# Seven products for eight in the first FFN products of a two-layer encoder step, with six load buffers, split weight sums, and a third slot in the last products

## The chip, the cores and the metric

The kernel runs on one core of one Trainium2 chip. The metric is device time in microseconds (us) from start to end of the launch; less is better. TensorE is called PE, VectorE DVE, ScalarE ACT, GpSimd POOL and SyncE SP.

## What is computed

Two groups of tokens (512 of a prompt, 8 x 16 of samples; together 640, as five tiles of 128) pass through two layers. Each layer is FFN, mixer, FFN, and each of these has an RMSNorm ahead of it and one behind it. Everything is fp32.

```
x = x + 0.5 * rmsnorm(swiglu(rmsnorm(x, g0), w_in, w_out), g1)
x = x + rmsnorm(mixer(rmsnorm(x, g2)), g3)          # layer 0: RG-LRU and FoX attention; layer 1: differential attention
x = x + 0.5 * rmsnorm(swiglu(rmsnorm(x, g4), w_in, w_out), g5)

swiglu(x, w_in, w_out):  g, u = split(x @ w_in);  return (silu(g) * u) @ w_out
# d_model 1024, d_ff 2816: w_in is 1024 x 5632, w_out is 2816 x 1024
```

So there are four FFNs, f = 0 to 3. The change touches them alone.

## The kernel before

**Precision.** Each fp32 product is made of three matmuls on fp32r parts: every operand is split into a high part (ACT copies it to fp32r, `act_hi`) and a low part (DVE subtracts the high part from the original, `dve_lo`), and PE adds low times high, high times low and high times high in PSUM.

**First products (A0 to A3, `pe_pairs`).** The 2816 hidden columns are 22 chunks of 128. For each chunk there are two weight tiles of 1024 x 128, one for the gate and one for the up half. The weights stand still in PE and the transposed tokens (`xT_hi`, `xT_lo`) stream past, in two pieces of 384 and 256 columns (tiles 0 to 2, tiles 3 and 4). That is 2 tiles x 8 blocks of the contraction x 3 parts x 2 pieces = 96 matmuls a chunk. ACT takes Silu of the gate's PSUM (`act_ffn`), DVE multiplies it with the up half's into the hidden state `hid` (`dve_ffn`). The weight tiles come through four load buffers `raw` (SP's queue, `sp_unit`) and two split slots (`w_slot`; the first two of a stage have slots apart).

**Last products (B0 to B3, `pe_ffn_out`).** Here a chunk of `hid` stands still and a row of 1024 weights streams past. A first group makes tiles 0 to 2 in 22 units (18 matmuls of 512 columns each, a loop), then a second group makes tiles 3 and 4 in 22 units (12 matmuls each, `pe_second_group`), while the norm of tiles 0 to 2 is taken on DVE, ACT and POOL (`dve_norm_first`, `act_norm_first`, `pool_norm`). Each unit's row and its piece of `hid` are split again, into one of two slots: unit u may be split once unit u - 2 is through PE. The last two units go through PE together (`pe_last_units`), so that tile 3 is ready before tile 4.

**Between stages.** With the last units running, ACT and DVE split the first tiles of the next stage, then finish the norm of tiles 3 and 4 (`act_norm_rest`, `dve_norm_rest`). PE transposes the normed tiles (`pe_xt`), ACT copies them out of PSUM as `xT_hi` and DVE subtracts for `xT_lo` (`act_xt`, `dve_xt`). The first products of a stage begin with tiles 0 to 2 while tiles 3 and 4 are still being normed.

Each engine runs its own list of instructions in order, with semaphores between engines; nothing reorders them.

## Time and profile before

| what | value |
|---|---|
| time, median of 3 runs | 2756.61 us (2749.81 to 2757.88) |
| the profiled execution: its own time, its span | 2743.6 us, 2741.5 us |
| PE busy | 2585.1 us, 94% of the span |
| DVE, ACT, POOL busy | 1146.5 us (42%), 865.4 us (32%), 120.1 us (4%) |
| granted clock of PE, mean | 0.979 |
| DMA | 260.93 MB, 95 GB/s over the span |

A busy PE in this profile is one that has matmuls in flight; their ends are modelled, so the distance from one start to the next tells what a matmul costs, not its own length. The profiled execution was 13 us shorter than the median of the runs.

### The profile page before, as it was taken

How to read it: one execution, taken by the hardware profiler on the slowest of the kernel's cores; microseconds unless marked ns; L12 is line 12 of the kernel's file. 1: busy time of each engine (PE TensorE's matmuls, PEld its weight loads, DVE VectorE, ACT ScalarE, POOL GpSimd, SP SyncE). 2: the span in 40 equal slices, each digit the busy share in tenths (PEclk: the TensorE clock that was granted, in tenths of full speed). 3: DMA queues.
4: the chain of work that ended last, by engine and by line, in shares of the span. 5: the costliest groups of instructions: out<-in, count | busy, mean ns of one | idle time of the engine just before them, and what ended most of it. 6: DMA issues, size and time to landing. Idle time of an engine off the chain costs nothing.

```text
span 2741.5 us, 38402 instructions
## 1 busy us (share of the span) xinstructions
PE 2585.1 (94%) x14963; PEld 2323.5 (85%) x14963; DVE 1146.5 (42%) x1739; ACT 865.4 (32%) x1427; POOL 120.1 (4%) x177
## 2 busy tenths in 40 slices
PE   6999999998889999999999999999996699999998
PEld 6999987886768999987799998777784479999986
DVE  3222246666556222235522223553247853222355
ACT  3112235344344222124422113442233442112243
...
GB/s 151 77 77 70 76 128 148 112 69 70 78 16 133 83 70 75 77 99 138 169 63 76 77 77 103 137 129 131 66 163 41 19 120 85 77 76 70 97 127 158
DMA packets 259061, 260.93 MB, mean 95 GB/s; under 512 B 25567, under 2 KB 213999, under 8 KB 258976
## 3 DMA queue, kind: packets, MB, share of 16 engines
...
## 4 chain that ended last, share of the span: by engine, by line
PE 83%; DVE 10%; ACT 3%; issue 2%; POOL 1%; DMA 1%; ACTq 0%; SPq 0%; DVEq 0%
PE ps L530 16%; PE ps L532 16%; PE ps L531 16%; PE ps L571 7%; PE ps L573 7%; PE ps L572 7%; PE ps L885 2%; DVE w_all L400 2%; PE ps L887 2%; PE ps L886 2%; ACT w_all L394 2%; PE ps L1361 1%; PE ps L1065 1%; PE ps L815 1%; DVE small L1420 1%
## 5 line engine op out<-in xcount | busy, mean ns | idle before, releaser
L400 DVE TENSOR_TENSOR w_all<-raw,w_all 128x1024 fp32r<-128x1024 f32 (+1 forms) x460 | 521.4, 1134 | 999.8 <-ACT w_all L394 679.3
L394 ACT ACTIVATE w_all<-raw 128x1024 fp32r<-128x1024 f32 (+1 forms) x460 | 453.8, 987 | 1521.2 <-PE ps L532 946.2
L530 PE MATMUL ps<-xT_hi,w_all 128*128 128x384 f32 (+1 forms) x2784 | 859.4, 309 | 2.0 <-DVE w_all L400 2.0
L532 PE MATMUL ps<-xT_hi,w_all 128*128 128x384 f32 (+1 forms) x2784 | 858.6, 308 | 0.0
L531 PE MATMUL ps<-xT_lo,w_all 128*128 128x384 f32 (+1 forms) x2784 | 858.5, 308 | 0.0
L530 PEld LDWEIGHTS ps<-xT_hi,w_all 128*128 128x128 f32 x2784 | 527.2, 189 | 2.2 <-DVE w_all L400 2.2
L531 PEld LDWEIGHTS ps<-xT_lo,w_all 128*128 128x128 f32 x2784 | 527.4, 189 | 0.0
L532 PEld LDWEIGHTS ps<-xT_hi,w_all 128*128 128x128 f32 x2784 | 527.2, 189 | 0.0
L571 PE MATMUL ps<-w_all 128*128 128x512 f32 x848 | 336.1, 396 | 17.4 <-DVE w_all L415 17.1
L572 PE MATMUL ps<-w_all 128*128 128x512 f32 x848 | 330.7, 390 | 0.0
L573 PE MATMUL ps<-w_all 128*128 128x512 f32 x848 | 330.5, 390 | 0.0
L481 DVE TENSOR_TENSOR arena<-silu,ps 128x384 f32 (+3 forms) x176 | 85.8, 488 | 369.8 <-PE ps L532 368.1
L571 PEld LDWEIGHTS ps<-w_all 128*128 128x128 f32 x848 | 159.1, 188 | 68.2 <-DVE w_all L415 35.0
L573 PEld LDWEIGHTS ps<-w_all 128*128 128x128 f32 x848 | 159.2, 188 | 34.3
L572 PEld LDWEIGHTS ps<-w_all 128*128 128x128 f32 x848 | 159.3, 188 | 30.4
L885 PE MATMUL ps<-w_all,xT_lo 128*128 128x512 f32 x354 | 141.9, 401 | 14.4 <-ACT tok L953 8.0
L886 PE MATMUL ps<-w_all,xT_hi 128*128 128x512 f32 x354 | 138.0, 390 | 0.0
L887 PE MATMUL ps<-w_all,xT_hi 128*128 128x512 f32 x354 | 138.0, 390 | 0.0
L716 POOL TENSOR_SCALAR small<-small 128x1 f32<-128x1 f32 x60 | 21.8, 364 | 2070.5 <-ACT scratch L662 2020.3
L885 PEld LDWEIGHTS ps<-w_all,xT_lo 128*128 128x128 f32 x354 | 66.4, 188 | 37.2 <-DVE w_all L400 17.1
L415 DVE TENSOR_TENSOR w_all<-arena,w_all 128x384 fp32r<-128x384 f32 (+1 forms) x176 | 85.4, 485 | 0.0
L410 ACT ACTIVATE w_all<-arena 128x256 fp32r<-128x256 f32 (+2 forms) x176 | 79.8, 453 | 0.0
...
## 6 DMA issues: line engine op xcount, KB each, us to landing
raw<-in_w_ffn_in SPq DMA_DIRECT2D x176, 512.0 KB, 3.8
raw<-in_w_ffn_out SPq DMA_DIRECT2D x176, 512.0 KB, 3.6
...
raw<-in_w_out_even SPq DMA_DIRECT2D x16, 512.0 KB, 3.6
raw<-in_w_out_odd SPq DMA_DIRECT2D x16, 512.0 KB, 3.7
gain<-in_norm_g POOLq DMA_DIRECT2D x12, 512.0 KB, 5.3
...
raw<-in_w_in_even SPq DMA_DIRECT2D x8, 512.0 KB, 4.0
```

The costliest lines, as they stand in the source:

```text
L394: return nc.scalar.activation(w_slot(u, it, n)[0], raw[:, u % 4, 0:n], ACT.Copy)
L400: return nc.vector.tensor_tensor(lo, raw[:, u % 4, 0:n], hi.bitcast(F32), ALU.subtract)
L481: nc.vector.tensor_tensor(dst, silu[:, half, 0:w], pair_bank(c, 1, half, w), ALU.mult).then_inc(h_done, 1)
L530: nc.tensor.matmul(dst, wl, xh, start=(k == 0), stop=False)
L531: nc.tensor.matmul(dst, wh, xl, start=False, stop=False)
L532: mm = nc.tensor.matmul(dst, wh, xh, start=False, stop=(k == KD - 1))
L571: nc.tensor.matmul(dst, xl, wh[:, cols], start=start, stop=False)
L572: nc.tensor.matmul(dst, xh, wl[:, cols], start=False, stop=False)
L573: mm = nc.tensor.matmul(dst, xh, wh[:, cols], start=False, stop=stop)
L885: nc.tensor.matmul(dst, xl, wh, start=(k == 0), stop=False)
L886: nc.tensor.matmul(dst, xh, wl, start=False, stop=False)
L887: return nc.tensor.matmul(dst, xh, wh, start=False, stop=(k == KD - 1))
```

## The change

The first products of an FFN become, for each chunk, a product of 2 x 2 blocks: the gate and the up tile are each halved along the contraction (four weight quarters of 512 x 128), and the tokens are halved along contraction and along tokens (four quarters of 512 x 320). Winograd's form of Strassen's scheme makes the four result blocks (gate and up, tokens 0 to 319 and 320 to 639) out of seven products of 4 blocks x 3 parts = 12 matmuls of 320 columns, so 84 matmuls a chunk. In PSUM the products that share a sum are added in place.

- **Token operands.** The transposed tokens are copied unsplit to `xs`; seven operands are made of them once for an FFN (B11, B21, B22 and the differences T1 to T4), each 128 x 1280, and each is split into `xb`. The `xT` and `tok` tiles now lie in the room of `xb`.
- **Weight operands.** For each chunk there are four sums of quarters, S1 to S4, made in place in the load buffers: S3 and S1 on POOL (`pool_sums`), S2 and S4 on DVE (`dve_sums`). Each of the seven operands (128 x 512) is split by ACT and DVE into a ring: four places apart for the first four, then five in turn (`w_ring`).
- **Results.** ACT copies three partial sums out of PSUM (P1, then P1+P6, then P1+P6+P7), DVE adds three times, ACT takes Silu twice, DVE multiplies twice; all of 320 columns.
- **Loads.** Six buffers serve the FFN's first products; the two new ones are the tile `gain`, whose norm gains are now loaded after the products.
- **Order.** `SEQUENCE` lists the 154 products of an FFN; every engine walks it. A product's operand is prepared up to five products ahead, its result is taken five steps later. The first products are no longer a loop.
- **Third slot.** In the second group of the last products the units use three slots in turn, one of them in `xb`, which is free by then (`late_slot`).

```diff
+SEQUENCE = [(name, j) for name in ("P1", "P2", "P5", "P6", "P7", "P4", "P3") for j in range(2)]
+SEQUENCE += [(name, j - back) for j in range(2, KF + 1)
+             for name, back in (("P1", 0), ("P5", 0), ("P4", 1), ("P6", 0), ("P2", 0), ("P3", 1), ("P7", 0))
+             if 2 <= j - back < KF]
+RING, AHEAD = 5, 4
+XOF = {"P1": "B11", "P2": "B21", "P3": "B22", "P4": "T4", "P5": "T1", "P6": "T2", "P7": "T3"}
...
+        def raw_buf(b):
+            return raw[:, b, :] if b < 4 else gain[:, b - 4, :]
...
+        def late_slot(u0, k, n=None):
+            g0, g1 = HALVES[1][0], TOK
+            if k % 3 == 0:
+                b = 0 if late_ffn(u0) in (1, 3) else 8
+                t = [xb[:, b + i].rearrange("p k n -> p (k n)").rearrange("p (a n) -> p a n", n=g1 - g0) for i in range(2)]
...
+        def act_hi_late(act, u0, k):
...
+            act.wait_ge(used, v - 2 if k else v - KF)
...
+        def act_operand(act, f, i):
+            name, j = SEQUENCE[i]
+            summed = {"P7": s3_done, "P5": s1_done, "P6": s2_done, "P3": s4_done}.get(name)
+            if summed is not None:
+                act.wait_ge(summed, KF * f + j + 1)
+            else:
+                pair_wait(act, f, j, 1 if name == "P4" else 0)
+            if i >= AHEAD + RING:
+                act.wait_ge(prod_mm, NPROD * f + i - RING + 1)
...
+            nc.scalar.activation(w_ring(i)[0], operand_raw(f, name, j), ACT.Copy).then_inc(op_hi, 1)
...
+        def pool_sums(pool, f, j):
+            a11, a12, a21, a22 = quarters(f, j)
+            g = KF * f + j
+            pool.wait_ge(op_lo, NPROD * f + PLACE["P1", j] + 1)
+            pair_wait(pool, f, j, 1)
+            nc.gpsimd.tensor_tensor(a11, a11, a21, ALU.subtract).then_inc(s3_done, 1)
+            pool.wait_ge(s3_done, g + 1)
+            nc.gpsimd.tensor_tensor(a21, a21, a22, ALU.add).then_inc(s1_done, 1)
...
         def dve_ffn(dve, f, p, nxt):
+            for i in range(AHEAD, NPROD + RING + 4):
+                if i == 4:
+                    dve.wait_ge(xt_hi, XT["pre%d" % (BEFORE[f] + 1)] + NT)
+                    dve_t(dve, f, "T1")
+                    dve_t(dve, f, "T3")
+                    dve_xb(dve, f, "T1")
+                if i == 5:
+                    dve_t(dve, f, "T2")
+                if i == 6:
+                    dve_xb(dve, f, "T2")
+                if i == 8:
+                    dve_t(dve, f, "T4")
+                    dve_xb(dve, f, "T3")
...
+                if i < NPROD:
+                    dve_operand(dve, f, i)
+                    dve_sums(dve, f, i)
...
+                if 0 <= i - RING < NPROD:
+                    dve_after(dve, f, i - RING)
+                if 0 <= i - RING - 3 < NPROD:
+                    dve_up(dve, f, i - RING - 3)
...
+        def pe_pairs_ffn(pe, f, meanwhile=None):
...
+                if i == AHEAD:
+                    pe_xt(pe, pre_, 3, 3)
+                    pe_xt(pe, pre_, 4, 4)
+                    pe.wait_ge(xt_hi, XT[pre_] + 4)
+                pe.wait_ge(op_lo, NPROD * f + i + 1)
+                if j == 0:
+                    pe.wait_ge(xb_lo_done, 7 * f + XB_ORDER.index(XOF[name]) + 1)
...
+                for k in range(HK):
...
+                    nc.tensor.matmul(dst, wl, xh[:, k, :], start=first, stop=False, skip_group_check=True)
+                    nc.tensor.matmul(dst, wh, xl[:, k, :], start=False, stop=False, skip_group_check=True)
+                    mm = nc.tensor.matmul(dst, wh, xh[:, k, :], start=False, stop=(k == HK - 1), skip_group_check=True)
```

**Where instructions stand.** The first place is DVE's list inside the first products. Before, two chunks are six rows: two products into `hid` (in `arena`) and one split a weight tile.

```order
L481 TENSOR_TENSOR arena<-silu,ps 128x384
L481 TENSOR_TENSOR arena<-silu,ps 128x256
L400 TENSOR_TENSOR w_all<-raw,w_all 128x1024
L481 TENSOR_TENSOR arena<-silu,ps 128x384
L481 TENSOR_TENSOR arena<-silu,ps 128x256
L400 TENSOR_TENSOR w_all<-raw,w_all 128x1024
```

After, one chunk in the middle of a stage is fourteen rows, of which the first twelve stand here with their waits (`gain` and `raw` are load buffers; L591 splits an operand, L616 and L620 are S2 and S4, L674, L667, L678 and L670 take results).

```order
L591 TENSOR_TENSOR w_all<-gain,w_all 128x512 [waits op_hi]
L674 TENSOR_TENSOR arena<-scratch,ps 128x320 [waits prod_mm,silu1_done]
L591 TENSOR_TENSOR w_all<-gain,w_all 128x512 [waits op_hi]
L616 TENSOR_TENSOR gain<-gain 128x512 [waits s3_done,op_lo]
L591 TENSOR_TENSOR w_all<-raw,w_all 128x512 [waits op_hi]
L667 TENSOR_TENSOR scratch<-scratch,ps 128x320 [waits prod_mm,p1_done]
L591 TENSOR_TENSOR w_all<-gain,w_all 128x512 [waits op_hi]
L678 TENSOR_TENSOR arena<-arena,ps 128x320 [waits prod_mm,u2_done]
L591 TENSOR_TENSOR w_all<-gain,w_all 128x512 [waits op_hi]
L620 TENSOR_TENSOR gain<-gain 128x512 [waits s2_done,op_lo]
L670 TENSOR_TENSOR arena<-arena,ps 128x320 [waits u3_done]
L591 TENSOR_TENSOR w_all<-raw,w_all 128x512 [waits op_hi]
```

One more split and the second product into `hid` follow. Between the first and the third row POOL makes S3 and S1, and ACT copies S1's high part: the third row waits for that.

The second place is PE's list at the start of a stage. Before, the transposes of tile 3 (`tok`) come after two products of 24 matmuls:

```order
L530 MATMUL ps<-xT_hi,w_apart 128x384
L531 MATMUL ps<-xT_lo,w_apart 128x384
L532 MATMUL ps<-xT_hi,w_apart 128x384
L815 MATMUL ps<-con,tok 128x128 x8
L530 MATMUL ps<-xT_hi,w_all 128x384
L531 MATMUL ps<-xT_lo,w_all 128x384
```

After, those of tiles 3 and 4 come together after four products of 12 matmuls, and the product behind them is P5, the first that needs tokens of both halves:

```order
L842 MATMUL ps<-xb,w_apart 128x320
L840 MATMUL ps<-xb,w_apart 128x320
L841 MATMUL ps<-xb,w_apart 128x320
L842 MATMUL ps<-xb,w_apart 128x320
L1195 MATMUL ps<-con,tok 128x128 x16
L840 MATMUL ps<-xb,w_all 128x320
L841 MATMUL ps<-xb,w_all 128x320
```

So the products that may run ahead of the late tiles are fewer matmuls than before (48 of 320 columns, where 72 of 384 stood before tile 4's transposes).

The third place is ACT's list where the second group of the last products begins. Before, each split of a row (L394) and of its piece of `hid` (L410) goes to `w_all`:

```order
L394 ACTIVATE w_all<-raw 128x1024 [waits used,raw_in2]
L410 ACTIVATE w_all<-arena 128x256
L662 ACTIVATE scratch,small<-ps 128x1024 [waits ss_x_done,m_mm]
L662 ACTIVATE scratch,small<-ps 128x1024 [waits ss_m_done,m_mm]
L394 ACTIVATE w_all<-raw 128x1024 [waits used,raw_in3]
L410 ACTIVATE w_all<-arena 128x256
```

After, the first unit and every third one go to `xb`, and the norm's rows (L1012) stand where they stood:

```order
L538 ACTIVATE xb<-raw 128x1024 [waits used,raw_in2]
L539 ACTIVATE xb<-arena 128x256
L1012 ACTIVATE scratch,small<-ps 128x1024 [waits ss_x_done,m_mm]
L1012 ACTIVATE scratch,small<-ps 128x1024 [waits ss_m_done,m_mm]
L538 ACTIVATE w_all<-raw 128x1024 [waits used,raw_in3]
L539 ACTIVATE w_all<-arena 128x256
```

## Rows read from the trace of the kernel before

**Rows 1.** The page: busy time of TensorE, and the chain's shares by engine.
```profile
PE 2585.1 (94%) x14963; PEld 2323.5 (85%) x14963; DVE 1146.5 (42%) x1739; ACT 865.4 (32%) x1427; POOL 120.1 (4%) x177
PE 83%; DVE 10%; ACT 3%; issue 2%; POOL 1%; DMA 1%; ACTq 0%; SPq 0%; DVEq 0%
```

**Rows 2.** Windows: busy us and instructions by engine, granted clock, DMA share, GB/s.
```profile
889.70:890.30 0.60, 0.60 (x9) 0.60 (x7) 0.60 (x1) 0.00 (x0) 0.18 (x1) 1.00 0.12 36
...
881.00:1192.00 311.00, 311.00 (x2127) 310.90 (x2126) 82.74 (x95) 67.01 (x97) 5.63 (x8) 1.00 0.27 79
1192.00:1282.00 90.00, 90.00 (x401) 74.51 (x400) 38.24 (x46) 34.33 (x48) 0.80 (x2) 1.00 0.40 123
1282.00:1356.00 74.00, 66.18 (x291) 51.39 (x290) 49.41 (x57) 38.81 (x59) 10.32 (x12) 1.00 0.54 166
2664.00:2735.00 71.00, 63.28 (x264) 48.08 (x262) 40.25 (x49) 31.09 (x47) 2.12 (x5) 1.00 0.49 156
```

**Rows 3.** Timeline of TensorE, one chunk of A0: start us, us, instruction.
```profile
101.07 0.34 PE L530 MATMUL ps<-xT_hi,w_all 128*128 128x384 f32 x1
...
105.23 0.28 PE L530 MATMUL ps<-xT_hi,w_all 128*128 128x256 f32 x1
...
108.10 0.34 PE L530 MATMUL ps<-xT_hi,w_all 128*128 128x384 f32 x1
...
115.13 0.34 PE L530 MATMUL ps<-xT_hi,w_all 128*128 128x384 f32 x1
```

**Rows 4.** Groups by line and shape: busy us and mean ns, idle before.
```profile
L400 DVE TENSOR_TENSOR w_all<-raw,w_all 128x1024 fp32r<-128x1024 f32 x382 | 467.7, 1225 | 869.8 <-ACT w_all L394 549.5 <-ACT w_all L410 320.0
L400 DVE TENSOR_TENSOR w_all<-raw,w_all 128x512 fp32r<-128x512 f32 x78 | 53.7, 690 | 130.0 <-ACT w_all L394 129.8
L394 ACT ACTIVATE w_all<-raw 128x1024 fp32r<-128x1024 f32 x382 | 404.7, 1060 | 1357.1 <-PE ps L532 934.4 <-PE ps L573 398.8 <-DVE arena L481 21.2
L394 ACT ACTIVATE w_all<-raw 128x512 fp32r<-128x512 f32 x78 | 49.1, 630 | 164.0 <-PE ps L887 152.3 <-PE ps L532 11.7
L481 DVE TENSOR_TENSOR arena<-silu,ps 128x384 f32 x72 | 39.9, 554 | 148.3 <-PE ps L532 148.3
L415 DVE TENSOR_TENSOR w_all<-arena,w_all 128x256 fp32r<-128x256 f32 x88 | 36.9, 419 | 0.0
L410 ACT ACTIVATE w_all<-arena 128x256 fp32r<-128x256 f32 x88 | 35.3, 401 | 0.0
```

**Rows 5.** Timeline of TensorE in B1's second group: waits before units, in brackets.
```profile
1289.26 0.50 PE L571 MATMUL ps<-w_all 128*128 128x512 f32 x1 [0.76 <-DVE w_all L415]
...
1296.39 0.50 PE L571 MATMUL ps<-w_all 128*128 128x512 f32 x1 [1.38 <-DVE w_all L415]
...
1350.26 0.50 PE L587 MATMUL ps<-w_all 128*128 128x512 f32 x1 [3.11 <-DVE w_all L415]
```

**Rows 6.** Timeline in B0's second group: GpSimd beside VectorE.
```profile
430.30 0.55 POOL L720 TENSOR_TENSOR small<-small 128x1 f32<-128x1 f32 x1
...
436.92 1.28 DVE L741 SCALAR_TENSOR_TENSOR x<-tok,small,x 128x1024 f32<-128x1024 f32 x1
437.13 2.94 POOL L720 TENSOR_TENSOR small<-small 128x1 f32<-128x1 f32 x1
```

**Rows 7.** Timeline at the start of A1: tile 4, and the table load.
```profile
889.33 1.28 DVE L751 SCALAR_TENSOR_TENSOR tok<-x,small,gain 128x1024 f32<-128x1024 f32 x1 [0.44 <-POOL small L720]
...
895.58 1.03 ACT L830 ACTIVATE xT_hi<-ps 128x1024 fp32r<-128x1024 f32 x1 [4.02 <-PE ps L815]
896.63 1.28 ACT L439 ACT_TABLE_LOAD   x1
```

**Rows 8.** Windows around a TensorE wait ahead of the odd output projection.
```profile
2184.00:2188.40 4.40, 0.00 (x0) 0.00 (x0) 2.37 (x3) 2.25 (x3) 2.40 (x3) 1.00 0.02 7
2188.50:2191.80 3.30, 0.00 (x0) 0.00 (x0) 3.30 (x4) 0.00 (x0) 0.54 (x1) 0.50 0.85 259
```

**Rows 9.** The page: loads of the first products' weights, size each, us to landing.
```profile
raw<-in_w_ffn_in SPq DMA_DIRECT2D x176, 512.0 KB, 3.8
```

More of the change, by code:

```diff
@@ L50 @@
 SLOT = D + HALVES[0][1]
[L53 to L54 removed]
+C_ID, C_UT, C_ONE, C_SL, C_NT, C_NC, C_UB = (i * P for i in (0, 1, 2, 4, 5, 6, 7))
+C_COS = 8 * P
 C_SIN = C_COS + NT * 8
@@ L161, in build_trunk @@
         ones = con[:, C_ONE:C_ONE + P]
-        raw_in = [sem("raw_in%d" % j) for j in range(4)]
+        raw_in = [sem("raw_in%d" % j) for j in range(6)]
         hi_done = sem("hi_done")
@@ L313, in sp_rows @@
                 full = rows // 4
-                with sp.Fori(0, full, 1) as it:
+                for j in range(4):
+                    sp_unit(sp, u0 + b * rows + j, None, wb[:, j, :])
+                with sp.Fori(1, full, 1) as it:
                     for j in range(4):
@@ L461, in act_ffn @@
+            act.wait_ge(prod_mm, NPROD * (f + 1))
+            act_hi_b(act, b0 + 1, None, 1, 0, free=False)
+            act.wait_ge(hid1_done, KF * (f + 1))
+            act.wait_ge(hid2_done, KF * (f + 1))
+            for k in range(2, 4):
                 act_hi_b(act, b0 + k, None, k, 0)
@@ L680, in act_norm_first, with act_xb_first @@
                     act_xt(act, "pre%d" % (p + 1), t, t)
-        def act_norm_rest(act, p, nxt):
-            if nxt:
+                    if t == 2:
+                        act_xb_first(act, p)
+        def act_xb_first(act, p):
+            f = FFN_PRE.get("pre%d" % (p + 1))
+            if f is not None:
+                act.wait_ge(xt_hi, XT["pre%d" % (p + 1)] + 3)
+                act.wait_ge(xt_ps, XT["pre%d" % (p + 1)] + 3)
+                act_xb(act, f, "B11")
+                act_xb(act, f, "B21")
+        def act_norm_rest(act, p, nxt):
+            f = FFN_PRE.get("pre%d" % (p + 1))
+            if f is not None:
+                for i in range(AHEAD):
+                    act_operand(act, f, i)
+            elif nxt:
                 for i in range(2):
@@ L764, in dve_norm_first, with dve_xb_first @@
                 if p < 5 and k == PE_TURN[rows][t] + 2:
-                    dve_xt(dve, "pre%d" % (p + 1), t, t)
-        def dve_norm_rest(dve, p, nxt):
-            if nxt:
+                    if "pre%d" % (p + 1) not in FFN_PRE:
+                        dve_xt(dve, "pre%d" % (p + 1), t, t)
+                    elif t == 2:
+                        dve_xb_first(dve, p)
+        def dve_xb_first(dve, p):
+            f = FFN_PRE["pre%d" % (p + 1)]
+            dve_xb(dve, f, "B11")
+            dve_xb(dve, f, "B21")
+        def dve_norm_rest(dve, p, nxt):
+            f = FFN_PRE.get("pre%d" % (p + 1))
+            if f is not None:
+                for i in range(AHEAD):
+                    dve_operand(dve, f, i)
+            elif nxt:
                 for i in range(2):
```

592 lines of the change are left out of this document (401 added, 191 removed).

## The prediction

> **What bounds the kernel now.** I read the page first. PE has matmuls in flight for 94% of the span, and 83% of the chain that ended last is PE's own work [rows 1]. So time goes only where PE does less, or waits less. Next I read windows, stage by stage. The first products of FFN 1 (A1) keep PE busy in all 311 us of their window, with DVE at 83 us and ACT at 67 us: this stage is PE's matmuls and nothing else. The first group of B1 fills its 90 us as well. The second group has PE busy for 66 of 74 us: here PE waits [rows 2].
>
> What a chunk costs comes from PE's timeline. From the first 384-column matmul at 101.07 to the next piece at 105.23 are 24 matmuls, 0.1733 us each; the 256-column ones take (108.10 - 105.23) / 24 = 0.1196 us. A chunk, 101.07 to 115.13, takes 14.06 us [rows 3]. 22 chunks make 309.3 us, so of a stage of 311 about 2 us go to its start, 1.2 of them to the transposes of tiles 3 and 4 (eight take 0.6 us [rows 2]).
>
> In the second group a unit is 12 matmuls of 512 columns. The first group's 22 units of 18 fill 90 us, or 0.227 us a matmul [rows 2], so a unit is worth 2.72 us, and 22 units with three tiles' transposes in between (1.8 us) 61.6 us. The window has 74. The timeline shows where the rest goes: waits of 0.76 and 1.38 us for a split early on, smaller ones before every second unit, and 3.11 us before the last two units [rows 5]. With two slots the split of a unit begins when the unit two before it leaves PE: 1.06 + 0.40 us on ACT, then 1.23 + 0.42 on DVE [rows 4], 3.1 us in all, against 2.72 us of PE's work on the unit between. The last pair must have both slots split before it starts, so all 3.1 us show.
>
> **The change, part by part.** *Matmuls.* A 320-column matmul stands midway between the measured ones: 0.1465 us (bounds 0.1196 and 0.1733). 84 of them are 12.31 us a chunk, 1.75 less than 14.06; 88 chunks give 154 us. Waits of PE's own list cost nothing before: its 0.1196 us rhythm ran through product boundaries unbroken [rows 3], and the new list asks for fewer instructions per microsecond.
>
> *Does the helping work fit into 12.3 us?* Per chunk ACT has seven copies of 512 columns (0.63 us) and five of 320 (between 0.40 and 0.63, say 0.45): 6.7 us. DVE has nine operations of 512 columns (0.69 us) and five of 320 (between 0.42 and 0.55, say 0.49): 8.7 us [rows 4]; less back to back, where the next begins some 0.08 us before the last one ends. Both fit. The order is tighter than the sum, since every engine works in order: after the low part of P1 POOL makes S3 and S1, then ACT copies P5's operand, and DVE's next split stands behind that copy. Let one sum on POOL cost g. A round of the helpers is then the low part of P1 0.69, two sums 2g, the copy 0.63, the low part 0.69, S2 0.69 (it waits for the low part), then four splits and S4 at about 0.62 each, four result operations at 0.41, and some 0.6 us of hand-overs between engines: 8.1 + 2g. The fifth, P4's product into `hid`, lies under POOL's work. That stays under 12.3 as long as g is below 2.1 us.
>
> The trace of before has no wide sum on POOL. Its nearest rows are a tensor-tensor of one column: 0.55 us alone, 2.94 us where it began just after a DVE operation and DVE went on without a gap [rows 6]. These are my bounds. I take g = 1.24, the 0.55 as fixed cost plus the 0.69 that DVE needs for 512 columns, because in the steady state DVE has only P4's product, which reads PSUM, until S1 is done. A round is then 10.6 us, PE stays the bound, and ring and look-ahead (four products, 7.0 us) cover P5's delay of 0.69 + 2g + 0.63 + 0.69, or 4.5 us.
>
> On POOL two rules of the Trainium skill speak against the change. Row first: POOL's small operation stretched from 0.55 to 2.94 us beside DVE [rows 6]. The page SBUF — State Buffer, section SBUF: two separate sides, says that a DVE operation with two SBUF inputs and a GpSimd operation that reads SBUF lock each other out for a whole instruction; the 2.94 us agree. The page GPSIMD Engine Reference, section 4.1 Engine selection, wants elementwise work on VectorE, because GpSimd is about twice as slow with two inputs; its 4497 ns for 2048 columns would make g an estimated 1.12 us and the round 10.3 us, with the sum below unchanged. No row here shows that price.
>
> *The start of each FFN.* B11 and B21 need tiles 0 to 2 only, so P1 and P2 of chunks 0 and 1 run first: 4 x 1.76 = 7.0 us. Before, 72 matmuls of 384 columns, 12.5 us, stood ahead of tile 4. Everything else needs all five tiles. After the last transposes: ACT's copy of tile 4, 1.03 us [rows 7]; DVE's T1 and T3, its low part of T1, and P5's low part. From 0.69 at 512 and 1.23 at 1024 columns [rows 4] an operation of 1280 columns costs 1.49 us (ACT 1.28, hidden beside T3). So 1.03 + 3 x 1.49 + 0.69 = 6.2, with hand-overs 6.5 us, in which PE has nothing. Then DVE cannot keep up: before P5 of chunk 1 it has S2, S4, T2 and a split (3.56 us against a product's 1.76), before P6 as much again, before P7 T4 and the low part of T3: 1.8 + 1.8 + 0.8 us of waiting. ACT loads Silu's table (1.28 us [rows 7]) and T4 ahead of a result that P7 needs: 1.5. Together 12.4 us. At A1 and A3, behind a mixer's short output projection, ACT and DVE make B11, B21 and four operands before they may finish tiles 3 and 4, and I add 2.6 us: 15.0. A gap of this length also costs clock: in 4.4 us of an idle PE the granted clock was still 1.00, in the next 3.3 us 0.50, which is 1.2 of 2.4 GHz [rows 8]. P5's first products will be slow, but they wait for DVE about as long; I add 1 us a start. The four starts cost 2 x 12.4 + 2 x 15.0 + 4 = 59 us. What the old starts lost beyond their transposes (4 x 0.8 = 3 us) comes back. The first products gain 154 - 59 + 3 = 98 us.
>
> *The third slot.* A unit's slot is free one unit earlier, so 3.1 us of splitting have 5.4 us, and the waits before every second unit and the 3.11 go. What stays is DVE's load at the beginning: nine norm operations of about 1.2 us and splits of 1.5 us in one list. Placed one after the other they reach units 1, 2 and 4 late by 0.3, 1.2 and 2.0 us, 3.7 in all with small change. A second group is then 61.6 + 3.7 = 65.3 instead of 74 (8.7 less, in B0 a little more); the last one, without transposes and next norm, 59.9 + 1.5 = 61.4 instead of 71 [rows 2]. Together 36 us.
>
> *Parts at nothing.* A load lands in 3.8 us [rows 9]; a buffer in six is asked for nine products, 15.8 us, ahead. SP holds chunk 2's tiles until the norm ahead is through, since two buffers are `gain`, but P1 of chunk 2 is the fifteenth product. The gains of the norms are loaded by POOL after the last operand, 90 us ahead of use. At the very start the parameters' transposes now come before the first product, where tile 2's copy and B11 are the later ones. If that cover were gone, each would cost one landing, some 4 us an FFN.
>
> **Sum.** 98 + 36 = 134 us from the profiled execution's 2743.6 gives 2610 us. That execution was 13 us below the median of the runs, so against the median of 2756.6 the forecast is 2623 us.
>
> **Rivals.** *A. POOL is the bound (slower).* If DVE keeps POOL out and a sum costs g = 2.94, a round is 14.0 us, the old chunk again: 88 x (14.0 - 12.3) = 149 us worse than forecast, 2771 us, slower than before by 0.5%. It decides against the change from g = 2.9 on; at 2.5 (13.1 us) the time is 2693. For it speaks the 2.94 us row; against it that DVE waits for that very sum in the steady state. The page rule above on elementwise work points to the same mechanism.
> *B. The starts cost twice as much*, because POOL's first four sums fall among T1 to T4 and lock against them, or the clock stays low: 59 us more, 2682 us. For it, that DVE has no gap there; against it, that P5 needs just two of these sums.
> *C. The third slot changes nothing*, since the norm and not the slot sets the waits: 36 us less gain, 2659 us. Against it, that the 3.11 us and the waits in B1's later units stand where no norm is.
> *D. The starts are half as costly*, 30 us better: 2593 us.
>
> **How the numbers follow.** Chances: forecast 0.58, A in full 0.04, A in part (g between 2.1 and 2.9) 0.10, B 0.12, C 0.06, D 0.10. The range takes in D, B and C: 2588 to 2686. The three runs spread by 0.3%, and about that is what can be told from no change. Only A in full ends within it or slower: faster 0.95, same 0.01, slower 0.04.
>
> **What the profile after would show.** Right: in the middle of an FFN's first products PE starts a 320-column matmul every 0.147 us and 84 in 12.3 us; POOL's 512-column sums below 2.1 us; one gap of 6 to 7 us on PE at each of four starts, waited for on DVE; no 3.1 us wait before the last units of B, and second groups of 65 us. Wrong: PE waiting in every chunk before P5 (rival A), or a start that costs 25 us (B).

## The result and the profile after

The changed kernel takes 2658.65 us in the median of four runs (2653.7 to 2662.37), the kernel before 2754.53 us in four runs beside them: a ratio of 0.9652, 95% interval 0.9626 to 0.9678. That is 96 us less, where 134 were forecast (2623 us, range 2588 to 2686). The profiled execution took 2654.97 us, with a span of 2653.2. The two profiled executions differ by 88.6 us (2743.6 to 2654.97); the medians differ by more, because the profiled execution before was 11 us shorter than its median and this one 4. The first products and the second groups, below, make 87 of the 88.6.

The page of the changed kernel: busy time by engine, and the chain that ended last by engine (to be set against [rows 1]).

```profile
PE 2452.6 (92%) x13907; PEld 2191.4 (83%) x13907; DVE 1585.2 (60%) x2643; ACT 1187.1 (45%) x2159; POOL 350.3 (13%) x353
PE 77%; DVE 14%; ACT 4%; issue 3%; POOL 2%; DMA 1%; ACTq 0%; DVEq 0%; POOLq 0%
```

PE has 133 us less to do and is still 92% busy, but its share of the chain falls from 83 to 77%: PE now waits in places where it did not, mostly for DVE. The windows say where: 100 us in the middle of A2's first products, then B1's first group, its second group, and the last second group (columns as in [rows 2]).

```profile
1500.00:1600.00 100.00, 99.80 (x681) 99.53 (x679) 63.20 (x113) 48.52 (x96) 19.30 (x16) 1.00 0.26 72
...
1152.00:1242.00 90.00, 89.77 (x397) 74.04 (x396) 39.19 (x48) 34.29 (x48) 0.69 (x2) 1.00 0.40 135
1242.60:1311.00 68.40, 64.41 (x290) 51.60 (x289) 48.16 (x57) 40.51 (x61) 10.32 (x12) 1.00 0.50 162
2584.30:2646.30 62.00, 60.82 (x265) 49.09 (x263) 39.70 (x49) 30.36 (x46) 2.31 (x6) 1.00 0.52 170
```

The middle is full: 681 matmuls in 100 us, 0.1468 us each. GpSimd's timeline shows the same rhythm, S3 and S1 of one chunk and S3 of the next, 12.31 us later:

```profile
1004.98 1.31 POOL L604 TENSOR_TENSOR gain<-gain 128x512 f32<-128x512 f32 x1 [9.65 <-DVE w_all L591]
1006.36 1.29 POOL L606 TENSOR_TENSOR gain<-gain 128x512 f32<-128x512 f32 x1
...
1017.29 1.31 POOL L604 TENSOR_TENSOR raw<-raw 128x512 f32<-128x512 f32 x1 [9.65 <-DVE w_all L591]
```

So the time is lost at the ends of the stages. These are PE's waits from P5(0) to chunk 2 in A2's timeline, then those at the end of A1's list (the bracket is the idle time and what ended it):

```profile
1328.03 0.60 PE L840 MATMUL ps<-xb,w_all 128*128 128x320 f32 x1 [7.17 <-DVE w_all L591]
1335.04 0.41 PE L840 MATMUL ps<-xb,w_all 128*128 128x320 f32 x1 [1.29 <-DVE w_all L591]
1340.76 0.39 PE L840 MATMUL ps<-xb,w_all 128*128 128x320 f32 x1 [1.93 <-ACT scratch L642]
1356.33 0.39 PE L840 MATMUL ps<-xb,w_all 128*128 128x320 f32 x1 [1.12 <-DVE scratch L678]
1363.72 0.38 PE L840 MATMUL ps<-xb,w_all 128*128 128x320 f32 x1 [1.88 <-ACT scratch L642]
```

```profile
1148.09 0.38 PE L840 MATMUL ps<-xb,w_all 128*128 128x320 f32 x1 [2.09 <-ACT arena L647]
1150.39 0.38 PE L840 MATMUL ps<-xb,w_all 128*128 128x320 f32 x1 [0.31 <-DVE arena L670]
```

The rows are P5(0), P6(0), P7(0), P5(2) and P7(2) (the number in brackets is the chunk); below, P4(21) and P3(21). The first three were forecast in kind. The other four were not.

A table makes this comparable. An FFN's 154 products at 12 x 0.1466 us are 270.9 us; whatever its 1848 matmuls take beyond that by their starts in PE's timeline is a loss, and it is put down to the products in whose place it falls (us, sum of the four FFNs, slow matmuls and the late transposes included):

| kernel | P5(0), with the gap before it | next 9 (P5(1) to P3(1)) | next 17 (from P1(2)) | next 119 | last 4 | all |
|---|---|---|---|---|---|---|
| forecast | 40 | 24 | 0 | 0 | 0 | 64 |
| changed kernel | 50.7 | 19.5 | 20.2 | 0.6 | 13.6 | 104.6 |
| e2, three sums on GpSimd | 49.8 | 20.8 | 34.8 | 71.4 | 14.4 | 191.2 |
| e3, four sums | 50.3 | 22.1 | 58.5 | 225.7 | 18.1 | 374.6 |
| e4, all sums on DVE | 48.0 | 20.8 | 5.4 | 0.4 | 18.7 | 93.2 |
| e5, end on ACT | 50.6 | 19.5 | 18.6 | 0.6 | 14.5 | 103.8 |
| e6, regular chunk 2 | 50.9 | 39.8 | 0.5 | 0.6 | 15.0 | 106.8 |
| e7, order at the start | 50.5 | 16.7 | 22.0 | 0.6 | 13.7 | 103.4 |
| e8, PE kept busy | 46.2 | 25.3 | 20.1 | 0.6 | 14.0 | 106.1 |
| e9, best | 45.0 | 19.6 | 5.4 | 0.4 | 3.4 | 73.7 |
| e10, best and order | 45.1 | 12.2 | 10.2 | 0.4 | 3.4 | 71.3 |
| e11, half of T1 to T4 | 47.5 | 12.9 | 15.8 | 0.6 | 13.5 | 90.2 |

(Forecast: 7.75 us at A0 and A2 and 10.35 at A1 and A3 up to P5(0), the late transposes included, 1 us each for the clock, 5.9 us each behind it. A0's first four products lose 1.6 to 2.8 us more in every one of these kernels, at half clock; they are left out, since A0 lost 3.2 us more than A1 in the kernel before too. The columns go by place in the list; in e6, whose list is another, the last two of the next 9 are P1 and P5 of chunk 2.) The changed kernel's 104.6 against 64 are the 41 us by which the first products gained 57 us (A0 314.6 to 298.1, A1 311.4 to 298.6, A2 311.4 to 295.1, A3 311.4 to 299.8) and not 98.

In B1's second group the wait of 3.11 us before the last units is gone; two early waits [rows 5], one of 1.37 us where DVE splits the next FFN's B11 and B21, and 0.39 us are left:

```profile
1249.19 0.50 PE L957 MATMUL ps<-w_all 128*128 128x512 f32 x1 [0.78 <-DVE w_all L546]
1256.33 0.50 PE L957 MATMUL ps<-w_all 128*128 128x512 f32 x1 [1.36 <-DVE w_all L546]
1285.60 0.50 PE L957 MATMUL ps<-w_all 128*128 128x512 f32 x1 [1.37 <-DVE w_all L546]
...
1305.32 0.50 PE L913 MATMUL ps<-w_all 128*128 128x512 f32 x1 [0.39 <-DVE xb L546]
```

The second groups take 66.9, 68.5, 66.9 and 62.1 us (75.5, 73.8, 73.8 and 71 before): 29.7 us less.

The costs of single operations came as estimated. By groups, the two halves of a split of 512 columns, on DVE and on ACT, and a result operation of 320 columns; then, from the list of DMA issues, the landing of a load:

```profile
L591 DVE TENSOR_TENSOR w_all<-raw,w_all 128x512 fp32r<-128x512 f32 x404 | 276.6, 687 | 240.2 <-ACT w_all L584 240.2
L584 ACT ACTIVATE w_all<-raw 128x512 fp32r<-128x512 f32 x404 | 250.2, 627 | 242.5 <-POOL raw L606 111.5 <-PE ps L842 84.8 <-DVE raw L616 46.3
L674 DVE TENSOR_TENSOR arena<-scratch,ps 128x320 f32<-128x320 f32 x88 | 42.3, 480 | 2.7 <-PE ps L842 2.7
...
raw<-in_w_ffn_in SPq DMA_DIRECT2D x120, 512.0 KB, 5.0
```

At the start GpSimd and DVE disturb one another. A2's timeline, GpSimd's first four sums, then DVE's norm operation on tile 4 (1.28 us in [rows 7]) and T1 with T3:

```profile
1317.35 1.28 POOL L604 TENSOR_TENSOR raw<-raw 128x512 f32<-128x512 f32 x1
1318.71 2.13 POOL L606 TENSOR_TENSOR raw<-raw 128x512 f32<-128x512 f32 x1
1320.81 1.26 POOL L604 TENSOR_TENSOR raw<-raw 128x512 f32<-128x512 f32 x1
1322.15 2.43 POOL L606 TENSOR_TENSOR raw<-raw 128x512 f32<-128x512 f32 x1
...
1317.42 2.29 DVE L1117 SCALAR_TENSOR_TENSOR tok<-x,small,gain 128x1024 f32<-128x1024 f32 x1 [0.72 <-POOL small L1086]
1321.96 3.97 DVE L718 TENSOR_TENSOR arena<-arena 128x1280 f32<-128x1280 f32 x2 [2.24 <-ACT arena L1210]
```

Windows of the stretch in which PE waits, of P5(0), and of DVE's list from T1 on:

```profile
1321.00:1328.00 7.00, 0.00 (x0) 0.00 (x0) 5.97 (x5) 3.56 (x5) 3.50 (x2) 0.80 0.53 148
1328.10:1331.20 3.10, 3.10 (x12) 3.07 (x12) 3.00 (x4) 0.31 (x1) 0.00 (x0) 0.50 0.00 0
...
1322.00:1347.00 25.00, 15.75 (x80) 14.87 (x81) 23.68 (x26) 14.85 (x24) 2.50 (x2) 0.80 0.15 39
```

PE's clock is at 0.50, 1.2 of 2.4 GHz, when P5(0) runs, and DVE is busy for 23.68 of 25 us. Whether the clock, the lock or DVE's amount of work costs the time is what the runs below separate.

In chunk 2, up to P7(2), it is another matter: DVE is busy for 9.90 of 18 us. It stands idle until ACT has copied the operands of P5(2) and P5(3), and ACT until GpSimd has made S1 for them (window, then DVE's and ACT's timeline in A2):

```profile
1347.00:1365.00 18.00, 14.90 (x99) 14.20 (x98) 9.90 (x18) 6.27 (x13) 5.20 (x4) 1.00 0.42 109
...
1351.25 0.69 DVE L591 TENSOR_TENSOR w_all<-gain,w_all 128x512 fp32r<-128x512 f32 x1 [3.06 <-ACT w_all L584]
1361.23 0.69 DVE L591 TENSOR_TENSOR w_all<-raw,w_all 128x512 fp32r<-128x512 f32 x1 [3.45 <-ACT w_all L584]
...
1350.58 0.63 ACT L584 ACTIVATE w_all<-gain 128x512 fp32r<-128x512 f32 x1 [3.52 <-POOL gain L606]
1360.57 0.63 ACT L584 ACTIVATE w_all<-raw 128x512 fp32r<-128x512 f32 x1 [3.88 <-POOL raw L606]
```

### The profile page after: what moved, and what is told of

Same layout as the page of the kernel before. It is cut to its first block, busy times and chain, and to the rows that moved or that the text cites. A ratio compares the mean times of both kernels' runs of the same rounds, so it can differ in the third digit from the quotient of the medians.

```text
span 2653.2 us, 37614 instructions
## 1 busy us (share of the span) xinstructions
PE 2452.6 (92%) x13907; PEld 2191.4 (83%) x13907; DVE 1585.2 (60%) x2643; ACT 1187.1 (45%) x2159; POOL 350.3 (13%) x353
## 4 chain that ended last, share of the span: by engine, by line
PE 77%; DVE 14%; ACT 4%; issue 3%; POOL 2%; DMA 1%; ACTq 0%; DVEq 0%; POOLq 0%
PE ps L840 12%; PE ps L841 12%; PE ps L842 12%; PE ps L898 5%; PE ps L899 5%; PE ps L900 5%; PE ps L1276 3%; PE ps L1278 2%; PE ps L1277 2%; PE ps L957 2%; PE ps L959 2%; PE ps L958 2%; DVE w_all L591 1%; DVE xb L705 1%; PE ps L1752 1%
## 5 line engine op out<-in xcount | busy, mean ns | idle before, releaser
L840 PE MATMUL ps<-xb,w_all 128*128 128x320 f32 x2400 | 752.7, 314 | 61.4 <-DVE w_all L591 31.7
L841 PE MATMUL ps<-xb,w_all 128*128 128x320 f32 x2400 | 748.8, 312 | 0.0
L842 PE MATMUL ps<-xb,w_all 128*128 128x320 f32 x2400 | 748.5, 312 | 0.0
L840 PEld LDWEIGHTS ps<-xb,w_all 128*128 128x128 f32 x2400 | 457.0, 190 | 71.1 <-issue 55.7
L841 PEld LDWEIGHTS ps<-xb,w_all 128*128 128x128 f32 x2400 | 457.3, 191 | 0.0
L842 PEld LDWEIGHTS ps<-xb,w_all 128*128 128x128 f32 x2400 | 457.0, 190 | 0.0
L491 DVE TENSOR_TENSOR w_all<-raw,w_all 128x1024 fp32r<-128x1024 f32 (+1 forms) x204 | 207.9, 1020 | 398.6 <-ACT w_all L501 211.9
L591 DVE TENSOR_TENSOR w_all<-raw,w_all 128x512 fp32r<-128x512 f32 x404 | 276.6, 687 | 240.2 <-ACT w_all L584 240.2
L485 ACT ACTIVATE w_all<-raw 128x1024 fp32r<-128x1024 f32 (+1 forms) x204 | 182.3, 895 | 482.3 <-PE ps L900 258.4
L584 ACT ACTIVATE w_all<-raw 128x512 fp32r<-128x512 f32 x404 | 250.2, 627 | 242.5 <-POOL raw L606 111.5
L591 DVE TENSOR_TENSOR w_all<-gain,w_all 128x512 fp32r<-128x512 f32 x196 | 134.7, 687 | 126.4 <-ACT w_all L584 126.4
L898 PE MATMUL ps<-w_all 128*128 128x512 f32 x528 | 205.9, 390 | 0.9 <-DVE w_all L506 0.9
L899 PE MATMUL ps<-w_all 128*128 128x512 f32 x528 | 205.5, 389 | 0.0
L900 PE MATMUL ps<-w_all 128*128 128x512 f32 x528 | 205.5, 389 | 0.0
L584 ACT ACTIVATE w_all<-gain 128x512 fp32r<-128x512 f32 x196 | 122.1, 627 | 131.3 <-POOL gain L606 62.7
L1276 PE MATMUL ps<-w_all,xT_lo 128*128 128x512 f32 x354 | 141.9, 401 | 14.7 <-ACT tok L1344 8.2
L898 PEld LDWEIGHTS ps<-w_all 128*128 128x128 f32 x528 | 99.1, 188 | 23.0 <-DVE w_all L506 2.6
L900 PEld LDWEIGHTS ps<-w_all 128*128 128x128 f32 x528 | 99.1, 188 | 20.7
```

The source lines that it names most:

```text
L491: return nc.vector.tensor_tensor(lo, raw[:, RAW[u][0], 0:n], hi.bitcast(F32), ALU.subtract)
L584: nc.scalar.activation(w_ring(i)[0], operand_raw(f, name, j), ACT.Copy).then_inc(op_hi, 1)
L591: nc.vector.tensor_tensor(lo, operand_raw(f, name, j), hi.bitcast(F32), ALU.subtract).then_inc(op_lo, 1)
L840: nc.tensor.matmul(dst, wl, xh[:, k, :], start=first, stop=False, skip_group_check=True)
L841: nc.tensor.matmul(dst, wh, xl[:, k, :], start=False, stop=False, skip_group_check=True)
L842: mm = nc.tensor.matmul(dst, wh, xh[:, k, :], start=False, stop=(k == HK - 1), skip_group_check=True)
```

## The experiments

The theory: PE's saving is whole in the middle of a stage, and what is missing is lost at its two ends. The rivals are named with each run. Unless said otherwise each is an edit of the changed kernel; 0.9652 is the ratio to set theirs against. The kernel before, run beside each set of runs, had medians from 2749.7 to 2756.4 us, so medians of different sets compare to some 5 us only; the ratios take that out.

**e1: two slots again.**

```diff
-            if k % 3 == 0:
+            if False:
...
-            at0 = (k % 3 - 1) * 2 * SLOT
+            at0 = (k % 2) * 2 * SLOT
...
-            act.wait_ge(used, v - 2 if k else v - KF)
+            act.wait_ge(used, v - 1)
```

> The second groups of the last products go back to two slots; nothing else changes. Theory (the third slot takes away the waits for splits): the 3.1 us wait before the last two units and the waits before every second unit come back, the four second groups take 74 us (the last 71) where the changed kernel has 66 to 69 (62): about 29 us more than the changed kernel, some 2688 us. Rival (the norm's work on DVE sets the waits, and the slot nothing): second groups stay at 66 to 69 us, 2659 us.

2694.14 us, ratio 0.9771 (0.9755 to 0.9787). The wait before the last units is back, and behind it the matmuls start 0.43 us apart and not 0.22:

```profile
1329.82 0.79 PE L913 MATMUL ps<-w_all 128*128 128x512 f32 x1 [3.11 <-DVE w_all L546]
1330.41 0.63 PE L914 MATMUL ps<-w_all 128*128 128x512 f32 x1
1330.83 0.63 PE L915 MATMUL ps<-w_all 128*128 128x512 f32 x1
```

The second groups take 75.5, 78.0, 73.8 and 72.7 us: 35.6 us more than with three slots. Rival C is out; in the changed kernel the third slot is worth some 35 us, somewhat more than the 29 that I had expected by then. Most of the 6 us between them is clock: behind the wait the last two units took 7.3, 8.6, 5.7 and 7.2 us in e1's four groups, where the kernel before took 7.4 us in one group (B0) and 5.7 in the others.

**e2 and e3: one and two more sums on GpSimd**, from chunk 2 on. (In e3 the loop runs twice, and a semaphore orders the two.)

```diff
             nc.gpsimd.tensor_tensor(a11, a11, a21, ALU.subtract).then_inc(s3_done, 1)
+            for _ in range(1 if j >= 2 else 0):
+                nc.gpsimd.tensor_tensor(w_all[:, 0:HK * P], a21, a22, ALU.add)
             pool.wait_ge(s3_done, g + 1)
```

> From chunk 2 on GpSimd makes one more sum of 512 columns between S3 and S1, into an unused piece of w_all; the result does not change. Theory (a round of the helpers is 8.1 us plus GpSimd's sums, 1.27 us each): 8.1 + 3.8 = 11.9 us, still under the 12.31 us of PE, so the steady state keeps 12.31 us a chunk and the time moves by less than 8 us (chunk 2's operand comes 1.3 us later in each FFN). Rival (the helpers are already level with PE): each of 80 chunks gets 1.27 us longer, about 100 us more.

> As the run with one more sum, but with two: four sums on GpSimd a chunk. Theory: a round of 8.1 + 4 x 1.27 = 13.2 us is 0.9 us over PE's 12.31; 80 chunks give about 72 us, 2731 us, and PE waits before P5 in every chunk. Rival (the helpers have far more room than the sum of the chain says, because ring and look-ahead cover it): no change, 2660 us. Rival (the extra sums lock against DVE): 160 us and more.

e2: 2748.78 us, ratio 0.9981 (0.9964 to 0.9997); e3: 2927.56 us, 1.0608 (1.0586 to 1.063). One sum more takes nearly the whole gain away: my theory of the helpers' round falls. In e2 PE waits in every chunk, before P5 (timeline of PE), and the period is 13.36 us:

```profile
1503.92 0.39 PE L842 MATMUL ps<-xb,w_all 128*128 128x320 f32 x1 [0.81 <-DVE arena L680]
1517.28 0.38 PE L842 MATMUL ps<-xb,w_all 128*128 128x320 f32 x1 [0.80 <-DVE scratch L680]
```

How much longer the round got is read from GpSimd's timeline. From S3's start to S1's end it takes 3.81 us in e2 and 2.67 in the changed kernel (1004.98 to 1007.65):

```profile
1509.21 1.30 POOL L604 TENSOR_TENSOR raw<-raw 128x512 f32<-128x512 f32 x1 [9.55 <-DVE w_all L591]
1510.47 1.29 POOL L606 TENSOR_TENSOR w_all<-raw 128x512 fp32r<-128x512 f32 x1
1511.72 1.30 POOL L608 TENSOR_TENSOR raw<-raw 128x512 f32<-128x512 f32 x1
```

13.36 less these 1.14 us leaves a round of 12.22 us in the changed kernel, not 10.6: a margin of 0.10 us a chunk. GpSimd's idle time before S3 says the same, 9.55 us here and 9.65 in the changed kernel; so does e3, where 5.17 us of sums go with the shorter period of 14.73. PE's rows above name the cause of the wait. It is not P5's operand but L680 (L678 in the changed kernel), the addition that takes P3's result of the chunk but one before out of the PSUM bank that P5 writes. On DVE it stands behind the splits of P5, P4 and P6, and so behind GpSimd's sums. The round closes through PE: P5 and P4 (3.5 us) must run before ACT may copy the next P1 into the ring; copy, split and hand-overs take 1.4 us, and from S3's start to that addition's end it is 6.8 us (1004.98 to 1011.76 in the changed kernel). These make 11.7 us; the rest of the 12.22 I put down to hand-overs between engines. My count had taken DVE's list alone.

In e3 the wait before P5 is 2.2 us, the period 14.7 or 16.3 us. The longer ones have matmuls at half clock (windows of 100 us in A2, e2 first, e3 second):

```profile
1500.00:1600.00 100.00, 93.54 (x627) 91.67 (x626) 60.72 (x108) 45.64 (x94) 26.67 (x21) 1.00 0.27 74
```

```profile
1600.00:1700.00 100.00, 86.97 (x544) 85.57 (x543) 48.26 (x86) 36.28 (x74) 34.74 (x28) 0.93 0.26 73
```

**e4: all four sums on DVE.** S3 and S1 of chunks 0 and 1 come before T1, later ones right behind P1's split; GpSimd's loop goes.

```diff
+        def dve_s31(dve, f, j):
...
+            nc.vector.tensor_tensor(a11, a11, a21, ALU.subtract).then_inc(s3_done, 1)
...
+            nc.vector.tensor_tensor(a21, a21, a22, ALU.add).then_inc(s1_done, 1)
...
                 if i == 4:
+                    dve_s31(dve, f, 0)
+                    dve_s31(dve, f, 1)
...
                     dve_sums(dve, f, i)
+                    if SEQUENCE[i][0] == "P1" and SEQUENCE[i][1] >= 2:
+                        dve_s31(dve, f, SEQUENCE[i][1])
...
-            for j in range(KF):
-                pool_sums(pool, f, j)
```

> S3 and S1 move from GpSimd to DVE; for chunks 0 and 1 they stand between the norm's last operation (tile 4) and T1, later right behind P1's low part. Theory (PE bounds the steady state, the starts are set by DVE's chain and partly by its lock with GpSimd): a sum costs DVE 0.69 us, the round is 8.1 + 1.4 = 9.5 us, 12.31 us a chunk stay; the norm's operation on tile 4 falls from 2.29 back to 1.28 us, T1 and T3 from 3.97 to 2.97 us, so the gap before P5 gets about 1.5 us shorter, and chunk 2's P5 comes without its 1.28 us wait: about 10 us less in all, 2649 us. Rival (the two sums on GpSimd are what lets DVE keep up): PE waits for DVE in every chunk, and the time is 50 us longer or more.

2649.35 us, ratio 0.9604 (0.9588 to 0.962): 9 us less than the changed kernel by the medians, 13 by the ratios, as the theory said. A2's timeline of DVE has the norm operation at 1.28 us again, a sum at 0.69, and T1 with T3 at 3.01:

```profile
1320.35 1.28 DVE L1130 SCALAR_TENSOR_TENSOR tok<-x,small,gain 128x1024 f32<-128x1024 f32 x1 [0.72 <-POOL small L1099]
1321.56 0.69 DVE L613 TENSOR_TENSOR raw<-raw 128x512 f32<-128x512 f32 x1
...
1324.21 3.01 DVE L727 TENSOR_TENSOR arena<-arena 128x1280 f32<-128x1280 f32 x2
```

Up to P5(0) this saves 1.4 to 2.0 us in A1 to A3; A0 loses 2.6, about what four sums of 0.69 take on DVE. The 17 products from P1(2) lose 5.4 and not 20.2 us, although DVE has more to do there: its splits no longer wait for GpSimd.

**e5: the last P7's copy first on ACT.**

```diff
-                if 0 <= i - RING < NPROD:
+                if 0 <= i - RING < NPROD and i != NPROD + 2:
                     act_after(act, f, i - RING)
...
                 if i == NPROD + 1:
+                    act_after(act, f, NPROD - 3)
```

> On ACT the copy of the last P7's sum moves ahead of the split for the first unit of the last products (both wait for that same P7). Theory (P4 of chunk 21 waits 2.1 to 2.6 us in each FFN because that copy stands behind the split's 1.06 + 0.51 us): the wait falls to some 0.6 us, 1.6 us or more an FFN, and up to 1.4 us of lowered clock behind it: 7 to 10 us in all, about 2650 us. Rival (the wait only moves to the first unit of the last products): no change, 2659 us.

2658.44 us, ratio 0.9659 (0.9638 to 0.9679): no change. P4(21) waits less, and the next product, P3(21), waits for it (PE's timeline, end of A1's list):

```profile
1147.55 0.38 PE L841 MATMUL ps<-xb,w_all 128*128 128x320 f32 x1 [0.62 <-ACT arena L647]
1151.53 0.38 PE L841 MATMUL ps<-xb,w_all 128*128 128x320 f32 x1 [1.99 <-DVE arena L670]
```

L670 is the addition of P7's sum. On DVE it stands behind the same unit's split. The wait moved by one product, not into the last products as the rival had it.

**e6: chunk 2's group made regular.**

```diff
-SEQUENCE = [(name, j) for name in ("P1", "P2", "P5", "P6", "P7", "P4", "P3") for j in range(2)]
+SEQUENCE = [(name, j) for name in ("P1", "P2", "P5", "P6", "P7", "P4", "P3") for j in range(2)][:-3]
+SEQUENCE += [("P3", 0)]
...
-             if 2 <= j - back < KF]
+             if 1 <= j - back < KF]
```

> P4 and P3 of chunk 1 leave the irregular beginning of the list and go into the group of chunk 2, where later chunks have them (B22 is made one step earlier). Theory (P7 of chunk 2 waits 2.05 us in each FFN, since the products that stand between P6 and P7 in later groups are missing there): that wait goes, about 8 us in all, 2651 us; P5's 1.28 us in chunk 2 may stay. Rival (the helpers have not caught up from the start by then, and the wait moves to another product of chunk 2): no change, 2659 us.

2659.65 us, ratio 0.9655 (0.9635 to 0.9674): no change, the rival's case. P7(2) waits no more, and chunk 2 loses 5.6 us in the four FFNs and not 20.2; the products before it lose 34.7 and not 19.5. Behind P5(0) the longest wait in A2's timeline is that of P7(0), for T3's low part; P5(2) still waits for the addition of P3's result:

```profile
1352.56 0.61 PE L841 MATMUL ps<-xb,w_all 128*128 128x320 f32 x1 [3.10 <-DVE xb L706]
...
1366.02 0.39 PE L841 MATMUL ps<-xb,w_all 128*128 128x320 f32 x1 [1.00 <-DVE scratch L679]
```

**e7: S4 and T4 later at the start.**

```diff
-            if name == ("P5" if j < 2 else "P2"):
+            if name == ("P7" if j < 2 else "P2"):
...
-        ACT_X = {4: ["T1"], 6: ["T2"], 8: ["T3"], 10: ["T4"], 12: ["B22"]}
+        ACT_X = {4: ["T1"], 6: ["T2"], 8: ["T3"], 12: ["T4"], 13: ["B22"]}
```

> At each start S4 of chunks 0 and 1 moves on DVE from the step of P5 to that of P7, and on ACT T4's copy (and B22's) moves behind the copy of P6's sum. Theory (P5(1) and P6(0) wait for DVE's list, P7(0) waits 2.1 us because ACT copies P6's sum after T4): P5(1) comes 0.7 us sooner and P6(0) 1.4, and P7(0) loses most of its 2.1 us: 2.5 to 3.5 us a start, 10 to 14 in all, about 2647 us. Rival (P5's first products run at half clock and P4(0) then waits for T4 instead): no change, 2659 us.

2661.76 us, ratio 0.9666 (0.9649 to 0.9683): no change. P5(1) and P6(0) lose most of their waits; P7(0) waits 2.54 us in A2 where it waited 1.93, for the same copy, and P1(2) 0.8.

**e8: TensorE kept busy through the gap.**

```diff
                     pe.wait_ge(xt_hi, XT[pre_] + 4)
+                    xh = xb[:, XB["B11"]]
+                    for _ in range(42):
+                        nc.tensor.matmul(bank(7, HT), w_ring(0)[0][:, 0:P], xh[:, 0, :], start=True, stop=True)
```

> During each start's wait TensorE runs 42 further matmuls of 320 columns (6.2 us) into a PSUM bank that is free then; they add nothing to the result. Theory (after the wait P5(0) runs at half clock, 1.46 us too slow, but DVE makes the operands of P5(1) and P6(0) no faster, so they wait instead): the granted clock at the starts rises to 1.00 and the time stays within 4 us, 2656 to 2659 us. Rival (the lowered clock costs what the slow products lose, 3 us a start with their successors): 12 us less, 2647 us.

2659.18 us, ratio 0.9652 (0.9632 to 0.9671): no change. The clock is 1.00 in the gap and in the products behind it (windows in A2):

```profile
1326.00:1333.00 7.00, 6.87 (x49) 6.61 (x47) 5.15 (x3) 3.67 (x5) 4.39 (x3) 1.00 0.55 150
1333.90:1338.00 4.10, 2.60 (x16) 2.34 (x17) 3.96 (x5) 1.23 (x2) 0.00 (x0) 1.00 0.00 0
```

PE is busy for 2.60 of 4.10 us there: P5(1) now starts 1.66 us behind PE's rhythm and not 0.26. The half clock behind the gap costs nothing.

**e9: all sums on DVE, both helpers reordered at the end.** e4 (A0's first four sums stay on GpSimd), e5, and on DVE:

```diff
-                if i == NPROD + 1:
+                if i == NPROD + 3:
                     dve.wait_ge(hid1_done, KF * f + 1)
...
                     dve_lo_b(dve, b0, None, 0, 0)
```

> All four sums on DVE as in e4 (in FFN 0 the sums of chunks 0 and 1 stay on GpSimd), and at the end of the list both the copy on ACT and the addition on DVE that the last P7 needs move ahead of the splits for the first unit of the last products. Theory: the gain of e4 (7 to 9 us against the changed kernel) stays, FFN 0's gap before P5 loses the 2.6 us that e4 added to it, and P4 and P3 of chunk 21 lose 2 us or more in each FFN, 8 to 12 us: some 2639 us. Rival (waits at the end move on into the last products as they moved in e5): 2647 us.

2630.93 us, ratio 0.9567 (0.9546 to 0.9588): faster than the changed kernel, and by 4 (by the ratios) to 8 us (by the medians) more than expected. The last four products lose 3.4 us, not 13.6 (or e4's 18.7); with both helpers changed the wait does not move on. One wait is left in A1 (PE's timeline):

```profile
1141.09 0.39 PE L854 MATMUL ps<-xb,w_all 128*128 128x320 f32 x1 [0.62 <-ACT arena L656]
```

**e10: e9 with another order at the start.** e7's edits, and besides:

```diff
-                    dve_t(dve, f, "T4")
                     dve_xb(dve, f, "T3")
+                    dve_t(dve, f, "T4")
...
-                if 0 <= i - RING - 2 < NPROD:
-                    act_silu(act, f, i - RING - 2)
+                for k in (i - RING - 2, i - RING - 5):
+                    if 0 <= k < NPROD and (k < 2 * RING) == (k == i - RING - 5):
+                        act_silu(act, f, k)
```

> As e9, and at each start S4 of chunks 0 and 1, T4's subtraction and copy and B22's copy stand later, T3's low part and the copy of P6's sum earlier (Silu of chunks 0 and 1 comes three steps later). Theory (with GpSimd's sums gone DVE has room in chunk 2, so what moves there is covered): the 4.6 us lost from P5(1) to P3(1) fall to about 2 us, chunk 2 loses no more than now: 10 us less than e9, some 2629 us. Rival (as in e7, DVE has no free time before the end of chunk 2, and the order changes nothing): as e9.

2629.57 us, ratio 0.9544 (0.9522 to 0.9567): not to be told from e9, so the rival is nearer. The table shows why: the nine products after P5(0) lose 7.4 us less, the seventeen behind them 4.8 us more.

**e11: half the work in T1 to T4.**

```diff
-            nc.vector.tensor_tensor(xs_quarter(*out), xs_quarter(*plus), xs_quarter(*minus),
+            o, a, b = (xs_quarter(*q)[:, :, 0:HT // 2] for q in (out, plus, minus))
+            nc.vector.tensor_tensor(o, a, b,
```

> The changed kernel, with T1 to T4 subtracted over half of their columns only (the other half keeps the unsubtracted tokens, so the output is another). An operation of 640 columns costs DVE about 0.83 instead of 1.49 us. Theory (DVE has no free time from tile 4 to the first sums of chunk 2, so its work sets the start, whatever the order): every start gets shorter by what DVE saves, 4 x 0.66 = 2.6 us; the gap before P5 by 1.3 us or more, the rest behind it: 10 us in all, about 2648 us. Rival (single hand-overs set the waits): no more than the two operations ahead of P5, 5 us.

2646.94 us, ratio 0.9621 (0.96 to 0.9643): 12 us less by the medians, 9 by the ratios, whose intervals overlap a little; the table is the firmer witness. The starts and chunk 2 lose 14.2 us less (47.5 + 12.9 + 15.8 against 50.7 + 19.5 + 20.2). Of these, 4.4 stand in chunk 2 and are nearly all clock: over its 17 products the granted clock is 0.95 on average in A0, A1 and A3 of the changed kernel, with some 1.5 us of matmuls at half rate behind P7(2)'s wait in each, and 1.00 in all four FFNs of e11. The other 9.8 are 2.5 us a start, where DVE was relieved of 2.6 by estimate. Less work shortens the start; e6, e7 and e8, which left the amount as it was, did not.

## Why the prediction was right, and where its sizes were off

**Matmuls: right.** 0.1465 us were worked out for a 320-column matmul, 0.1466 are measured; 84 take 12.31 us, as said, and the 119 products in the middle of each stage lose 0.6 us in all four FFNs.

**The helpers: the conclusion held, the step under it failed.** A sum on GpSimd costs 1.30 us (1.24 taken), so "POOL's 512-column sums below 2.1 us" came true, outside the starts. But "8.1 + 2g" and "PE stays the bound as long as g is below 2.1" are wrong: by e2 and e3 the round is 12.22 us, and the bound was g = 1.30 + 0.05 us. The failed piece is "ring and look-ahead (four products, 7.0 us) cover P5's delay". P5 waits for its bank, not only for its operand, and the addition that frees the bank stands three splits further down DVE's list. Rival A was thus 0.05 us a sum away and not 0.9, and I gave it too little chance. That PE stayed the bound in the middle of the stages was luck, not foresight.

**GpSimd beside DVE.** GpSimd's sum shows 1.26 to 1.33 us where DVE does nothing or reads PSUM, 2.13 and 2.43 us beside DVE's operations with two SBUF inputs, and the norm operation 2.29 for 1.28. The forecast took nothing for this; for the starts that was wrong. The Trainium skill, page SBUF — State Buffer, section SBUF: two separate sides, states that a DVE operation with two SBUF inputs and a GpSimd operation that reads SBUF shut each other out for a whole instruction, whichever starts first; the rows agree: S3 ends at 1318.63, the norm operation, begun 0.07 us behind S3, at 1319.71, and S1 at 1320.84, one after the other. The Trainium skill, page GPSIMD Engine Reference, section 4.1 Engine selection, wants elementwise work on VectorE; e4 agrees, with 9 us less. From the figure for 2048 columns on that page of the Trainium skill a sum was an estimated 1.12 us; 1.30 is measured.

**The starts: right in kind, too small.** 59 us were taken for the four. By the table the part up to P5(0) is 10.7 us dearer than forecast, the part to P7 4 us cheaper. The gap itself came as forecast, 6.6 to 7.2 us for 6.5. Some 7 of the 10.7 us lie ahead of it, where PE's transposes of tiles 3 and 4 wait for DVE's norm operations (in A1 1.17 and 1.90 us); the forecast had 2.6 us for that at A1 and A3 and nothing at A0 and A2. e4 gives the lock some 5.4 us of the 10.7 (A1 to A3); that is rival B's mechanism at a tenth of its price. P5(0)'s half clock adds 1.46 us a start for the 1 assumed, but nothing is won without it (e8), since DVE is what PE would wait for instead.

**What was not foreseen: chunk 2 and the end of the list.** The forecast let the start end at P7. Up to P7 of chunk 1 DVE has next to no free time: e6, e7 and e8 move or cover single waits and leave the sum as it is; e11 takes work out of DVE and the sum falls. But the loss goes on to P7(2), 20.2 us in the four FFNs, and there DVE is little more than half busy. It waits for GpSimd's sums for P5(2) and P5(3). Later chunks have the same wait (3.05 us at 1008.34) at no cost to PE; that chunk 2 has no products in hand to cover it is read from the list, not tested. The sums themselves were tried: the same 17 products lose 5.4 us with all sums on DVE (e4), 20.2 with two on GpSimd, 34.8 with three (e2) and 58.5 with four (e3). Some 4 of the 20.2 are clock that falls behind P7(2)'s wait. The last products lose 13.6 us because two results of the last P7 stand behind the next stage's first split, one on ACT and one on DVE; e5 undid one and gained nothing, e9 both and gained 10 us. Together: 10.7 - 4 + 20.2 + 0.6 + 13.6 = 41 us.

**The third slot: right.** 36 us forecast, 29.7 seen between the two kernels, 35.6 in e1. The early waits came as forecast (3.3 us in B0 for 3.7). What the forecast lacked is the wait of 0.39 us before the last units of each group and the one of 1.37 us in B1 where DVE splits B11 and B21; and three tiles' transposes cost some 2.8 us a group, not 1.8.

**Parts at nothing.** A load lands in 5.0 us and not 3.8; no wait of PE names one.

What stays open: up to P5(0), e9 still loses 45 us. That DVE's chain from tile 4 to P5's split makes it is read from the timeline; no run shortened it by more than the lock and half of T1 and T3.
